# Attention scores of two shares side by side: heads of both parities in alternation, in a two-block transformer kernel

## The chip, the cores and the metric

The kernel runs on one core of a Trainium2 chip. A core has a matrix engine (TensorE, "PE" in the profile, with its weight loads shown apart as "PEld"), a vector engine (VectorE, DVE), a scalar engine (ScalarE, ACT), GpSimd (POOL) and a queue engine (SyncE, SP) that issues DMAs. TensorE writes its results to PSUM, of which the kernel uses eight banks of 512 fp32 columns. Each engine works through its own list of instructions in order, and they wait for one another on semaphores. The metric is the device time of one execution in microseconds (us).

## What is computed

The model is a stack of two blocks over 256 tokens of width 1024. The first has an RG-LRU layer and a GLA layer, each followed by a gated FFN. The second has four layers, each of FFN, mixer, FFN; the mixers are DSA, FoX, MLA and DSA again. The change concerns DSA and FoX. Cut to what matters:

```python
def dsa_mixer(x, w_in, w_out, cos_p, sin_p):
    q, k, v, qi, ki, wi = split(x @ w_in)          # 16 heads of 64; index: 8 heads of 64
    # indexer: I[t,s] = sum_h w[t,h] relu(qi[t,h] . ki[s]); keep the top 64 causal keys
    dots = einsum('bqhd,bkd->bqhk', qi, ki) * 64**-0.5
    idx_score = where(causal, einsum('bqh,bqhk->bqk', wi, relu(dots)), -inf)
    _, sel = top_k(idx_score, 64)
    logits = einsum('bqhd,bqkhd->bhqk', q, k[sel]) * 64**-0.5
    return einsum('bhqk,bqkhd->bqhd', softmax(logits), v[sel]) @ w_out

def fox_mixer(x, w_in, b_f, w_out):
    q, k, v, f = split(x @ w_in)                   # 16 heads of 64
    cum = cumsum(log_sigmoid(f + b_f))             # per head
    s = (q . k) * 64**-0.5 + cum[query] - cum[key]
    return softmax(where(causal, s, -inf)) @ v @ w_out
```

## The kernel before

**Projections.** Weights stream from HBM in 428 units of 128x2048 numbers. For each unit ScalarE rounds it (`whi`, L1025), GpSimd forms the remainder (`wlo`, L2256), and TensorE multiplies both with the activations (`hTh`, `hTl`): three fp32r matmuls for each product. L448 is the form with 256 columns, L510 that with 512. They take most of the time.

**Attention in shares.** The 16 heads times two query tiles are cut into 16 shares of two heads. Share `i` is `order[name][i]` = (t, h0) with heads h0 and h0+2, so both heads of a share have the same parity. Heads of even number lie in partitions 0 to 63 of `q` and `k`, those of odd number in 64 to 127 (`heads`). A score matmul is therefore of 64 rows; its columns are 128 for query tile t=0 and 256 for t=1. For DSA the shares go by tile (eight of t=0, then eight of t=1), for FoX two of t=0 and two of t=1 in turn. In both, shares 2m and 2m+1 have the same t and heads of opposite parity.

**A step** (`step`, L765) is `score` of share s (L714, matmuls at L723, for FoX also the bias matmul at L727 on the same 64 partitions) and `turn_share` of share s-3 (L731, fp32 transposes at L737). There are 19 steps. They stand between the projection's matmuls: `rows_units` or `chan` calls the next one after every 5, 6 or 18 of them (`beside`, `every`). After `started` steps the rest comes in `finish`, in an order written out in `tail`, with `weigh` (probabilities times values, L752) and `turn_heads_sum` (L762), and then the output projection.

**What follows a step.** VectorE's `biased` scales and masks a share and so frees its PSUM bank (L2020, FoX: two instructions L2016), then takes the row maximum (L2024). ScalarE's `exps` makes the exponentials (L1303), TensorE transposes them, and ScalarE's `turned_share` copies the result out (L1033) and frees the bank. Score banks are handed out in turn from `cb` (two banks) for DSA and from `mb` (two banks) for FoX; transposes always use `mb`. So FoX scores and transposes share two banks. `claim` makes TensorE wait until a bank's last user has freed it.

**The indexer** (`index`, L816) has 16 parts of one 64-row matmul (L825), part i being head i//2, tile i%2, one after every third L510 matmul. Each goes through a ReLU on ScalarE (L1360) and a multiply-add on VectorE (L2110), which frees the bank; they too use the two `cb` banks.

Of the kernel before, what the change touches and what calls it, by code (L numbers as in the profile page):

```python
# [14 lines left out]
P = 128  # L15
# [143 lines left out]
def program(nc, W, A2, xin, pvd, cnd, normg, adab, lng, lnb, glag, out):  # L159
    ctx = ExitStack()  # L160
    with ctx:
# [52 lines left out]
        ident = cst("ident")  # L214
# [105 lines left out]
        lag = {"dsa0": 3, "dsa1": 3, "fox": 3, "mla": 3}  # L320
# [35 lines left out]
        def steps(name):  # L356

            g = lag[name]
            return [(s if s < 16 else None, s - g if s >= g else None) for s in range(16 + g)]


        started = {"dsa0": 11, "dsa1": 11, "fox": 19, "mla": 0}

        def tail(name):


            S, W, T = (lambda *a: [("step", i) for i in a]), (lambda *a: [("weigh", i) for i in a]), lambda t, g: [("turn", t, g)]
# [12 lines left out]
            return (W(0, 1, 2, 3) + S(11) + W(4, 5, 6, 7) + S(12) + T(0, 0) + S(13) + T(0, 1) + S(14),  # L380
                    S(15) + W(8, 9) + S(16) + W(10, 11) + S(17) + W(12, 13) + T(1, 0) + S(18) + W(14, 15) + T(1, 1))


        def tensor_program(q):
# [330 lines left out]
            def score(name, i, kind, ready):  # L715

                t, h0 = order[name][i]
                nk = 128 * (t + 1)
                to = claim(bank(kind), (name, "s", i))
                ready()  # L720
                for j in range(2):
                    hd = h0 + 2 * j
                    ins = pe.matmul(to[:, j * 256:j * 256 + nk], qs[name](hd)[:, t * 128:t * 128 + 128], ks[name](hd)[:, 0:nk],  # L723
                                    start=True, stop=name != "fox")
                    if name == "fox":
                        r = 64 * (hd % 2)
                        ins = pe.matmul(to[:, j * 256:j * 256 + nk], ident[r:r + 64, r + hd:r + hd + 1].broadcast_to([64, P]),  # L727
                                        f_l[r:r + 64, 0:nk], start=False, stop=True)
                ins.then_inc(*up(s_mm, ("full", (name, "s", i))))
# [35 lines left out]
            def step(name, s, kind, ready):  # L765
                i, p = steps(name)[s]
                if i is not None:
                    score(name, i, kind, lambda: ready(i))
                if p is not None:
                    turn_share(name, p)  # L770
# [27 lines left out]
            def dsa(n, name):  # L798
# [18 lines left out]
                def index():  # L817
                    for i in range(16):
                        hd, t = i // 2, i % 2
                        o, nk = 64 * (hd % 2), 128 * (t + 1)  # L820
                        to = claim(bank("cb"), (name, "i", i))
                        q.wait_ge(*on(name, "qiT", t, 0))
                        for tt in range(t + 1):
                            q.wait_ge(*on(name, "kiT", tt, 0))
                        ins = pe.matmul(to[:, 0:nk], d_qiT3[o:o + 64, hd // 2, t * 128:t * 128 + 128], d_kiT[o:o + 64, 0:nk],  # L825
                                        start=True, stop=True)
                        ins.then_inc(*up(s_mm, ("full", (name, "i", i))))
                        yield
# [29 lines left out]
                rows_units(hi2, *hk, ready, (name, "q"), last=True, beside=beside, every=3)  # L858
# [153 lines left out]
        def scalar_program(q):  # L1012
# [302 lines left out]
            def step(name, s):  # L1315
                i, p = steps(name)[s]
                if i is not None:
                    exps(name, i)
                if p is not None:
                    turned_share(name, p)  # L1320
# [21 lines left out]
            def dsa(n, name):  # L1342
# [13 lines left out]
                def index(parts):  # L1356
                    for i in parts:
                        q.wait_ge(*on("full", (name, "i", i)))
                        to = view((name, "i", i))[:, 0:128 * (i % 2 + 1)]
                        ac.activation(to, to, ACT.Relu, scale=0.125).then_inc(*up(s_ac, (name, "relu", i)))  # L1360
# [44 lines left out]
            def fox(n, name):  # L1405
# [45 lines left out]
                step(name, 18)  # L1451
# [99 lines left out]
        def vector_program(q):  # L1551
# [475 lines left out]
            def step(name, s):  # L2027
                i, _ = steps(name)[s]
                if i is not None:
                    biased(name, i)  # L2030
# [48 lines left out]
            def dsa(n, name):  # L2079
# [20 lines left out]
                def index(parts):  # L2100
                    for i in parts:
                        hd, t = i // 2, i % 2
# [4 lines left out]
                        else:  # L2107
                            q.wait_ge(*on(name, "iadd", i - 2))
# [11 lines left out]
                for t in range(2):  # L2120
# [4 lines left out]
                    q.wait_ge(*on(name, "iadd", 14 + t))  # L2125
# [342 lines left out]
```

## Time and profile before

| what | value |
|---|---|
| runs of the kernel before | 2913.04, 2912.8, 2909.71 us; median 2912.8 |
| the profiled execution | 2909.76 us, of which the span of instructions 2908.0 us |
| mean granted TensorE clock | 0.973 |
| busy share: PE / DVE / ACT / POOL | 95% / 30% / 46% / 68% |
| score matmuls of 64 rows | DSA (L723) 128 records, FoX (L723 and L727) 128 records |
| index matmuls L825 | 64 records |
| score and transpose stages | DSA 1045 to 1110 and 2634 to 2698 us, FoX 1532 to 1630 us |

The page gives busy time for each engine; matmuls overlap, so "busy" there is an upper figure for TensorE. Where a step costs something is read in the timeline: it lists instructions by their start, merged where one follows another of its kind ("x2"), and the distance from one start to the next is what an instruction takes in the stream. An fp32 matmul leaves two records, so "L723 ... x4" is the two matmuls of one DSA share.

### The profile page before, as it was taken

The page shows a single profiled execution, that of the slowest core. Times are in us where ns is not written, and L with a number is a line of the kernel's source. Part 1 is how long each engine was busy: PE and PEld are TensorE (multiplying, and loading weights), DVE is VectorE, ACT ScalarE, POOL GpSimd, SP SyncE. Part 2 cuts the span into 40 slices and gives each one's busy share as a digit, 9 for nine tenths or more (in the row PEclk, how much of TensorE's full clock was granted, in tenths as well). Part 3 has the DMA queues.
Part 4 walks back from the last instruction along what each step waited for, and adds up shares of the span by engine and source line. Part 5 has one row for each costly group of instructions (what it writes and reads, how often), then busy time and mean ns, then how long its engine had stood idle before and what let it go on. Part 6 is the DMA issues. An engine that isn't in the chain of part 4 may idle for free.

```text
span 2908.0 us, 41508 instructions
## 1 busy us (share of the span) xinstructions
PE 2757.7 (95%) x17914; PEld 2476.6 (85%) x17914; DVE 861.8 (30%) x1464; ACT 1326.3 (46%) x1599; POOL 1970.9 (68%) x432
## 2 busy tenths in 40 slices
PE   7789988799999999999999999999799999999998
PEld 4678876699899679999988899998689999977998
DVE  6666569343200342011022200201241020143201
ACT  3554443445543454344455533433654344445443
POOL 3557754377787655878875588787538878764785
PEclk8989989899999999999999999999899999999999
DMA  8567755265555433555544355554415555443453
GB/s 326 194 258 271 253 208 192 80 215 177 184 194 183 152 131 132 188 188 194 184 179 149 121 204 188 189 188 161 158 58 212 183 199 184 169 154 116 166 184 114
DMA packets 80410, 522.12 MB, mean 180 GB/s; under 512 B 8908, under 2 KB 9292, under 8 KB 24420
## 3 DMA queue, kind: packets, MB, share of 16 engines
q1 hardware_dynamic: 80228, 519.47, 49.8%
q8 instruction: 142, 2.33, 0.3%
q14 instruction: 40, 0.33, 0.0%
HBM read 518.38 MB, written 1.05 MB: 179 GB/s over the span
## 4 chain that ended last, share of the span: by engine, by line
PE 81%; DVE 9%; ACT 6%; POOL 2%; DMA 2%; issue 1%; SPq 0%; DVEq 0%; ACTq 0%
PE cb L448 40%; PE acc L510 14%; PE acc L471 14%; PE cb L562 3%; ACT whi L1025 2%; POOL wlo L2256 2%; DVE AR L1736 1%; PE acc L752 1%; PE cb L723 1%; PE acc L448 1%; DMA raw<-in_w 1%; PE mb L737 1%; PE acc L422 1%; DVE hTl L1686 1%; ACT AR L1114 1%
## 5 line engine op out<-in xcount | busy, mean ns | idle before, releaser
L2256 POOL TENSOR_TENSOR wlo<-raw,whi 128x2048 fp32r<-128x2048 f32 x428 | 1970.7, 4613 | 913.4 <-ACT whi L1025 813.7
L1025 ACT ACTIVATE whi<-raw 128x2048 fp32r<-128x2048 f32 x428 | 817.9, 1913 | 910.0 <-PE cb L448 602.7
L448 PE MATMUL cb<-hTh,whi 128*128 128x256 f32 x3328 | 946.6, 284 | 7.9 <-DVE cb L1745 7.9
L448 PE MATMUL cb<-hTl,whi 128*128 128x256 f32 x3328 | 942.5, 283 | 0.0
L448 PE MATMUL cb<-hTh,wlo 128*128 128x256 f32 x3328 | 942.4, 283 | 0.0
L448 PEld LDWEIGHTS cb<-hTh,whi 128*128 128x128 f32 x3328 | 639.1, 192 | 16.7 <-issue 13.8
L448 PEld LDWEIGHTS cb<-hTl,whi 128*128 128x128 f32 x3328 | 639.2, 192 | 3.8 <-issue 1.2
L448 PEld LDWEIGHTS cb<-hTh,wlo 128*128 128x128 f32 x3328 | 639.3, 192 | 0.0
L471 PE MATMUL acc<-whi,ARR 128*128 128x512 f32 x1312 | 367.0, 391 | 2.7 <-DVE ARR L1686 2.7
L1749 DVE SCALAR_TENSOR_TENSOR cb<-cb,AR 128x512 f32<-128x512 f32 x80 | 56.0, 700 | 979.3 <-PE cb L448 979.3
L471 PEld LDWEIGHTS acc<-whi,ARR 128*128 128x128 f32 x1312 | 241.4, 188 | 50.7 <-issue 4.8
L471 PE MATMUL acc<-wlo,ARR 128*128 128x512 f32 x656 | 202.6, 390 | 0.0
L510 PE MATMUL acc<-whi,hTh 128*128 128x512 f32 x464 | 148.4, 400 | 13.4 <-POOL wlo L2256 8.3
L510 PE MATMUL acc<-wlo,hTh 128*128 128x512 f32 x464 | 154.5, 398 | 0.0
L510 PE MATMUL acc<-whi,ARR 128*128 128x512 f32 x512 | 143.5, 398 | 3.3 <-DVE ARR L1686 3.3
L471 PEld LDWEIGHTS acc<-wlo,ARR 128*128 128x128 f32 x656 | 123.2, 188 | 26.5
L510 PE MATMUL acc<-whi,hTl 128*128 128x512 f32 x464 | 142.9, 388 | 0.0
L510 PEld LDWEIGHTS acc<-whi,ARR 128*128 128x128 f32 x512 | 97.1, 191 | 25.7 <-issue 6.1
L1686 DVE TENSOR_TENSOR ARR<-cb,ARR 128x512 fp32r<-128x512 f32 x105 | 72.3, 689 | 153.7 <-ACT ARR L1033 153.7
L510 PEld LDWEIGHTS acc<-whi,hTh 128*128 128x128 f32 x464 | 80.2, 194 | 33.2 <-issue 15.6
L1736 DVE SCALAR_TENSOR_TENSOR AR<-cb,pv,AR 128x255 f32<-128x255 f32 (+1 forms) x144 | 66.1, 480 | 132.4 <-ACT AR L1114 129.9
L510 PEld LDWEIGHTS acc<-wlo,hTh 128*128 128x128 f32 x464 | 84.1, 192 | 16.7
(299 smaller groups left out, 3088.6 us busy)
## 6 DMA issues: line engine op xcount, KB each, us to landing
raw<-in_w SPq DMA_DIRECT2D x436, 1024.0 KB, 4.8
AR<-in_a SPq DMA_DIRECT2D x80, 512.0 KB, 5.5
gb<-in_lng SPq DMA_DIRECT2D x12, 512.0 KB, 5.7
gb<-in_lnb SPq DMA_DIRECT2D x12, 512.0 KB, 6.5
gb<-in_normg SPq DMA_DIRECT2D x8, 512.0 KB, 6.4
x<-in_x SPq DMA_DIRECT2D x1, 1024.0 KB, 9.4
out<-x SPq DMA_DIRECT2D x2, 512.0 KB, 2.7
cn<-in_cn SPq DMA_DIRECT2D x1, 560.0 KB, 7.2
```

Of the source, the lines that this page charges most:

```text
L422: ins = pe.transpose(to[:, j * 128:j * 128 + 128], src[:, t, i * 128:i * 128 + 128], ident)
L448: ins = pe.matmul(to[:, j * 256:j * 256 + 256], a[:, w], y[:, k, :], start=k == 0 and m == 0, stop=k == 7 and m == 2)
L471: ins = pe.matmul(acc[:, 2 * t + c, 0:c1 - c0], xs[y], a[:, kk * width + c0:kk * width + c1], start=first and kk == 0 and m == 0, stop=las ...
L510: ins = pe.matmul(acc[:, 2 * t + c, 0:c1 - c0], xs[y], a[:, kk * width + c0:kk * width + c1], start=first and i == 0 and kk == 0 and m == ...
L562: ins = pe.matmul(to[:, i * 256:i * 256 + 256], y[:, k, tk], a[:, k * 256:k * 256 + 256], start=k == 0 and m == 0, stop=k == 7 and m == 2)
L723: ins = pe.matmul(to[:, j * 256:j * 256 + nk], qs[name](hd)[:, t * 128:t * 128 + 128], ks[name](hd)[:, 0:nk], start=True, stop=name != "fox")
L737: ins = pe.transpose(to[:, m * 128:m * 128 + 128], s3[:, j, kt * 128:kt * 128 + 128], ident)
L1025: ac.activation(whi[i % NH][:, :], raw[u % NR][:, :], ACT.Copy).then_inc(*up(s_hi, ("hi", i)))
L1686: dv.tensor_tensor(dst, src, high.bitcast(F32), ALU.subtract).then_inc(*up(s_dv, *names))
L1736: dv.scalar_tensor_tensor(out=to[:, a + sh:a + 256], in0=view(key)[:, a:a + 256 - sh], scalar=pvc(w, (2 - sh) * 44 + c0 + j), in1=to[:, a ...
L1749: dv.scalar_tensor_tensor(out=view(key1), in0=view(key1), scalar=0.5, in1=tmp(0, p % 2), op0=ALU.mult, op1=ALU.mult).then_inc(*up(s_dv, (" ...
L2256: po.tensor_tensor(wlo[i % NH][:, :], raw[(i + NADA) % NR][:, :], whi[i % NH][:, :].bitcast(F32), ALU.subtract).then_inc(*up(s_lo, ("lo", i)))
```

## The change

The diff, cut to its core:

```diff
-        lag = {"dsa0": 3, "dsa1": 3, "fox": 3, "mla": 3}
+        paired = {"dsa0": True, "dsa1": True, "fox": True, "mla": False}
...
         def steps(name):
-            g = lag[name]
-            return [(s if s < 16 else None, s - g if s >= g else None) for s in range(16 + g)]
-        started = {"dsa0": 11, "dsa1": 11, "fox": 19, "mla": 0}
+            if paired[name]:
+                return [((s, s + 1) if s % 2 == 0 and s < 16 else (), (s - 3, s - 2) if s % 2 and s > 2 else ())
+                        for s in range(18)]
+            return [((s,) if s < 16 else (), (s - 3,) if s > 2 else ()) for s in range(19)]
+        def index_part(i):
+            return i // 4 * 2 + i % 2, i // 2 % 2
+        started = {"dsa0": 11, "dsa1": 11, "fox": 18, "mla": 0}
...
-            def score(name, i, kind, ready):
-                t, h0 = order[name][i]
-                nk = 128 * (t + 1)
-                to = claim(bank(kind), (name, "s", i))
-                ready()
+            def scores_of(name, parts, kind, ready):
+                to = [claim(bank(kind), (name, "s", i)) for i in parts]
+                for i in parts:
+                    ready(i)
                 for j in range(2):
-                    hd = h0 + 2 * j
-                    ins = pe.matmul(to[:, j * 256:j * 256 + nk], qs[name](hd)[:, t * 128:t * 128 + 128], ks[name](hd)[:, 0:nk],
-                                    start=True, stop=name != "fox")
+                    for i, o in zip(parts, to):
+                        t, h0 = order[name][i]
+                        hd, nk = h0 + 2 * j, 128 * (t + 1)
+                        ins = pe.matmul(o[:, j * 256:j * 256 + nk], qs[name](hd)[:, t * 128:t * 128 + 128], ks[name](hd)[:, 0:nk],
+                                        start=True, stop=name != "fox")
...
-                ins.then_inc(*up(s_mm, ("full", (name, "s", i))))
+                ins.then_inc(*up(s_mm, *[("full", (name, "s", i)) for i in parts]))
...
-                    for i in range(16):
-                        hd, t = i // 2, i % 2
-                        o, nk = 64 * (hd % 2), 128 * (t + 1)
-                        to = claim(bank("cb"), (name, "i", i))
+                    for i0 in range(0, 16, 2):
+                        to = [claim(bank("cb"), (name, "i", i)) for i in (i0, i0 + 1)]
+                        for i in (i0, i0 + 1):
+                            hd, t = index_part(i)
...
-                rows_units(hi2, *hk, ready, (name, "q"), last=True, beside=beside, every=3)
+                rows_units(hi2, *hk, ready, (name, "q"), last=True, beside=beside, every=6)
```

Even steps now hold the scores of two shares, odd steps the transposes of two; `scores_of` claims both banks of the ring at once, goes through the two heads of each share in alternation of the shares, and reports both as full after its last matmul. The indexer takes two heads of one tile together, after every sixth matmul. VectorE and ScalarE follow the same steps; their instructions are the same, the multiply-adds of the indexer in the new order of parts. MLA, GpSimd's list and the DMA queue's list are as before. `tail` loses its last step for DSA.

TensorE in FoX, `mb0` and `mb1` being the two banks, L448 (after: L455) the matmuls of a channel unit. Before, share 3 with the transposes of share 0:

```order
L448 MATMUL cb<-hTh,wlo1 128x256
L723 MATMUL mb1<-AR 128x256 [waits s_dv]
L727 MATMUL mb1<-AR,cn 128x256
L723 MATMUL mb1<-AR 128x256
L727 MATMUL mb1<-AR,cn 128x256
L737 MATMUL mb0<-cn,AR 128x128 [waits s_ac,s_dv]
L737 MATMUL mb0<-cn,AR 128x128
L448 MATMUL cb<-hTh,whi1 128x256
```
After, shares 4 and 5 in one piece:

```order
L455 MATMUL cb<-hTh,wlo2 128x256
L732 MATMUL mb0<-AR 128x128 [waits s_ac]
L732 MATMUL mb1<-AR 128x128
L739 MATMUL mb0<-AR,cn 128x128
L739 MATMUL mb1<-AR,cn 128x128
L732 MATMUL mb0<-AR 128x128
L732 MATMUL mb1<-AR 128x128
L739 MATMUL mb0<-AR,cn 128x128
L739 MATMUL mb1<-AR,cn 128x128
L455 MATMUL cb<-hTh,whi2 128x256
```
The score rows of two shares have moved together and alternate in bank, and so in parity. The transposes have moved to a place of their own, 18 channel matmuls behind; here are those of shares 2 and 3:

```order
L455 MATMUL cb<-hTh,wlo2 128x256
L749 MATMUL mb0<-cn,AR 128x128 [waits s_dv]
L749 MATMUL mb0<-cn,AR 128x128 x3
L749 MATMUL mb1<-cn,AR 128x128 [waits s_dv]
L749 MATMUL mb1<-cn,AR 128x128 x3
L455 MATMUL cb<-hTh,whi2 128x256
```
They have moved behind the next pair's scores and claim the two banks that these have just filled, each with a wait for VectorE.

TensorE in the indexer of the first DSA layer, between L510 (after: L517) matmuls. Before:

```order
L825 MATMUL cb<-AR 128x256 [waits s_ac,s_dv]
L510 MATMUL acc<-whi3,hTh 128x512 x2
L510 MATMUL acc<-wlo3,hTh 128x512
L825 MATMUL cb<-AR 128x128 [waits s_dv]
L510 MATMUL acc<-wlo3,hTh 128x512
L510 MATMUL acc<-whi3,hTl 128x512 x2
L825 MATMUL cb<-AR 128x256 [waits s_dv]
```
Each part stands alone, three matmuls from the next. After:

```order
L838 MATMUL cb<-AR 128x128 x2
L517 MATMUL acc<-whi3,hTh 128x512 x2
L517 MATMUL acc<-wlo3,hTh 128x512 x2
L517 MATMUL acc<-whi3,hTl 128x512 x2
L838 MATMUL cb<-AR 128x256 [waits s_ac,s_dv]
L838 MATMUL cb<-AR 128x256
```
Parts have moved from every third matmul to two after every sixth, both of one width.

TensorE in the tail of the first DSA layer, up to the output projection at L510 (after: L517). Before, from the first `turn_heads_sum` (L762), with shares 13 and 14 at L723 and the transposes of shares 10 and 11 at L737:

```order
L762 MATMUL mb0<-cn,AR 128x128 [waits s_dv,s_ac]
L762 MATMUL mb0<-cn,AR 128x128 x3
L723 MATMUL cb<-AR 128x256 [waits s_dv]
L723 MATMUL cb<-AR 128x256
L737 MATMUL mb1<-cn,AR 128x128 [waits s_ac]
L737 MATMUL mb1<-cn,AR 128x128 x3
L762 MATMUL mb0<-cn,AR 128x128 [waits s_dv]
L762 MATMUL mb0<-cn,AR 128x128 x3
L723 MATMUL cb<-AR 128x256 x2
L737 MATMUL mb1<-cn,AR 128x128 [waits s_ac]
L737 MATMUL mb1<-cn,AR 128x128 x3
L510 MATMUL acc<-whi1,hTh 128x512 [waits s_lo,s_hi]
```
Scores and transposes stand between the two `turn_heads_sum`. After (L732 scores, L749 transposes, L774 `turn_heads_sum`), from the scores of shares 12 and 13:

```order
L732 MATMUL cb<-AR 128x256 [waits s_dv]
L732 MATMUL cb<-AR 128x256 x3
L774 MATMUL mb0<-cn,AR 128x128 [waits s_dv,s_ac]
L774 MATMUL mb0<-cn,AR 128x128 x3
L749 MATMUL mb1<-cn,AR 128x128 [waits s_ac]
L749 MATMUL mb1<-cn,AR 128x128 x3
L749 MATMUL mb0<-cn,AR 128x128 [waits s_dv]
L749 MATMUL mb0<-cn,AR 128x128 x3
L774 MATMUL mb1<-cn,AR 128x128 [waits s_ac]
L774 MATMUL mb1<-cn,AR 128x128 x3
L732 MATMUL cb<-AR 128x256 x4
L517 MATMUL acc<-whi1,hTh 128x512 [waits s_lo,s_hi]
```
Shares 12 and 13 have moved ahead of the first `turn_heads_sum`, 14 and 15 behind the second, and the transposes of shares 10 and 11 both stand between the two, the second of them with a wait for VectorE.

## Rows read from the trace of the kernel before

**Rows 1.** The page, part 4: the chain that ended last, by engine.
```profile
PE 81%; DVE 9%; ACT 6%; POOL 2%; DMA 2%; issue 1%; SPq 0%; DVEq 0%; ACTq 0%
```

**Rows 2.** Timeline of TensorE, DSA, 128-column scores: start, us, engine, line, tiles, count.
```profile
1046.97 0.62 PE L510 MATMUL acc<-whi,hTh 128*128 128x512 f32 x2
1047.52 0.71 PE L723 MATMUL cb<-AR 64*128 64x128 f32 x4
1048.16 0.73 PE L510 MATMUL acc<-wlo,hTh 128*128 128x512 f32 x2
1048.72 0.62 PE L510 MATMUL acc<-whi,hTl 128*128 128x512 f32 x2
1049.19 0.62 PE L510 MATMUL acc<-whi,hTh 128*128 128x512 f32 x2
```

**Rows 3.** Timeline of TensorE, FoX, a 256-column share between channel matmuls.
```profile
1540.92 0.28 PE L448 MATMUL cb<-hTh,wlo 128*128 128x256 f32 x1
1541.13 0.70 PE L723 MATMUL mb<-AR 64*128 64x256 f32 x2
1541.66 0.59 PE L727 MATMUL mb<-AR,cn 64*128 64x256 f32 x2
1542.10 0.59 PE L723 MATMUL mb<-AR 64*128 64x256 f32 x2
...
1543.05 0.39 PE L448 MATMUL cb<-hTh,whi 128*128 128x256 f32 x1
1543.27 0.28 PE L448 MATMUL cb<-hTl,whi 128*128 128x256 f32 x1
```

**Rows 4.** Timeline of TensorE, indexer: the 128-column parts of two heads.
```profile
994.70 0.48 PE L825 MATMUL cb<-AR 64*128 64x128 f32 x2
...
997.53 0.48 PE L825 MATMUL cb<-AR 64*128 64x128 f32 x2
```

**Rows 5.** Timeline of TensorE, FoX: matmuls of 64 columns in a run.
```profile
1608.45 7.26 PE L752 MATMUL acc<-z,AR 128*128 128x64 f32 x64
1615.54 1.04 PE L762 MATMUL mb<-cn,AR 128*128 128x128 f32 x8
```

**Rows 6.** Timeline of ScalarE in the indexer; the bracket is idle time before, and its releaser.
```profile
1001.70 1.02 ACT L1033 ACTIVATE AR<-acc 128x1024 f32<-128x1024 f32 x1 [1.75 <-DVE acc L2077]
...
1005.37 0.37 ACT L1360 ACTIVATE cb<-cb 128x256 f32<-128x256 f32 x1 [1.25 <-PE cb L825]
```

**Rows 7.** Timeline of VectorE, FoX, one 256-column share.
```profile
1543.16 0.88 DVE L2016 SCALAR_TENSOR_TENSOR AR<-mb,AR,cn 128x256 f32<-128x256 f32 x2 [4.64 <-PE mb L727]
1544.07 0.69 DVE L2024 TENSOR_REDUCE sm<-AR 128x2 f32<-128x512 f32 x1
```

**Rows 8.** Timeline of TensorE, first DSA layer, share 8 to the output projection.
```profile
1063.26 1.13 PE L723 MATMUL cb<-AR 64*128 64x256 f32 x4
...
1079.89 0.66 PE L737 MATMUL mb<-cn,AR 128*128 128x128 f32 x4 [1.03 <-ACT AR L1033]
...
1084.03 1.11 PE L737 MATMUL mb<-cn,AR 128*128 128x128 f32 x4 [0.74 <-ACT AR L1033]
1084.80 1.20 PE L510 MATMUL acc<-whi,hTh 128*128 128x512 f32 x2
```

**Rows 9.** Timeline of ScalarE in the same tail.
```profile
1072.30 1.90 ACT L1025 ACTIVATE whi<-raw 128x2048 fp32r<-128x2048 f32 x1
1074.10 1.01 ACT L1033 ACTIVATE z<-acc 128x1024 f32<-128x1024 f32 x1
1075.01 0.50 ACT L1303 ACTIVATE AR<-AR,sm 128x256 f32<-128x256 f32 x1
...
1075.99 0.58 ACT L1033 ACTIVATE AR<-mb 128x512 f32<-128x512 f32 x1
```

**Rows 10.** Timeline of VectorE in the same tail, one share.
```profile
1073.44 0.69 DVE L2020 SCALAR_TENSOR_TENSOR AR<-cb,AR 128x512 f32<-128x512 f32 x1
1074.17 0.69 DVE L2024 TENSOR_REDUCE sm<-AR 128x2 f32<-128x512 f32 x1
```

**Rows 11.** Windows: length, busy of PE, PEld, DVE, ACT, POOL, granted clock, DMA.
```profile
1082.00:1092.00 10.00, 9.26 (x30) 6.61 (x28) 3.73 (x6) 5.20 (x16) 0.00 (x0) 0.51 0.10 42
2672.50:2679.50 7.00, 6.58 (x19) 4.71 (x20) 3.35 (x5) 3.12 (x10) 0.00 (x0) 0.52 0.00 0
```

More of the change, by code:

```diff
@@ L713, in gla @@
                 out_units(n, lh, ll, ready)
-            def score(name, i, kind, ready):
-                t, h0 = order[name][i]
-                nk = 128 * (t + 1)
-                to = claim(bank(kind), (name, "s", i))
-                ready()
-                for j in range(2):
-                    hd = h0 + 2 * j
-                    ins = pe.matmul(to[:, j * 256:j * 256 + nk], qs[name](hd)[:, t * 128:t * 128 + 128], ks[name](hd)[:, 0:nk],
-                                    start=True, stop=name != "fox")
-                    if name == "fox":
-                        r = 64 * (hd % 2)
-                        ins = pe.matmul(to[:, j * 256:j * 256 + nk], ident[r:r + 64, r + hd:r + hd + 1].broadcast_to([64, P]),
-                                        f_l[r:r + 64, 0:nk], start=False, stop=True)
-                ins.then_inc(*up(s_mm, ("full", (name, "s", i))))
+            def scores_of(name, parts, kind, ready):
+                to = [claim(bank(kind), (name, "s", i)) for i in parts]
+                for i in parts:
+                    ready(i)
+                for j in range(2):
+                    for i, o in zip(parts, to):
[3 more added lines that the diff above has]
+                                        start=True, stop=name != "fox")
+                    if name == "fox":
+                        for i, o in zip(parts, to):
+                            t, h0 = order[name][i]
+                            hd, nk = h0 + 2 * j, 128 * (t + 1)
+                            r = 64 * (hd % 2)
+                            ins = pe.matmul(o[:, j * 256:j * 256 + nk], ident[r:r + 64, r + hd:r + hd + 1].broadcast_to([64, P]),
+                                            f_l[r:r + 64, 0:nk], start=False, stop=True)
+                ins.then_inc(*up(s_mm, *[("full", (name, "s", i)) for i in parts]))
             def turn_share(name, i):
@@ L765, in step @@
             def step(name, s, kind, ready):
[L766 to L769, printed above, removed]
+                scores, turns = steps(name)[s]
+                if scores:
+                    scores_of(name, scores, kind, ready)
+                for p in turns:
                     turn_share(name, p)
@@ L817, in index @@
                 def index():
-                    for i in range(16):
-                        hd, t = i // 2, i % 2
-                        o, nk = 64 * (hd % 2), 128 * (t + 1)
-                        to = claim(bank("cb"), (name, "i", i))
[L822 to L827, printed above, removed]
+                    for i0 in range(0, 16, 2):
+                        to = [claim(bank("cb"), (name, "i", i)) for i in (i0, i0 + 1)]
+                        for i in (i0, i0 + 1):
+                            hd, t = index_part(i)
+                            o, nk = 64 * (hd % 2), 128 * (t + 1)
+                            q.wait_ge(*on(name, "qiT", t, 0))
+                            for tt in range(t + 1):
+                                q.wait_ge(*on(name, "kiT", tt, 0))
+                            ins = pe.matmul(to[i % 2][:, 0:nk], d_qiT3[o:o + 64, hd // 2, t * 128:t * 128 + 128],
+                                            d_kiT[o:o + 64, 0:nk], start=True, stop=True)
+                        ins.then_inc(*up(s_mm, ("full", (name, "i", i0)), ("full", (name, "i", i0 + 1))))
                         yield
@@ L1315, in step @@
             def step(name, s):
-                i, p = steps(name)[s]
-                if i is not None:
+                scores, turns = steps(name)[s]
+                for i in scores:
                     exps(name, i)
-                if p is not None:
+                for p in turns:
                     turned_share(name, p)
@@ L2027, in step @@
             def step(name, s):
-                i, _ = steps(name)[s]
-                if i is not None:
+                for i in steps(name)[s][0]:
                     biased(name, i)
```

11 lines of the change are left out of this document (5 added, 6 removed).

## Prediction

> **What bounds the kernel now.** I read the chain that ended last first: 81% of it is TensorE [rows 1]. The timelines of the changed stages then show how: between the projection's matmuls the other engines are rarely waited for, and the time of a score is what its matmuls, and the gaps around them, take out of TensorE's stream. Only the tail of a DSA layer has waits, 1.03 us on ScalarE among them [rows 8]. So a saving in TensorE's stream should reach the end, unless a new wait takes it back.
>
> **The gap around a score.** DSA, 128 columns: from the L510 pair at 1046.97 to the one at 1048.72 are 1.75 us [rows 2]. Two L510 pairs in them take 0.47 each (1048.72 to 1049.19). That leaves 0.81 for four records of scores. What is a record? In FoX, 256 columns, two records take 0.44 (1541.66 to 1542.10) [rows 3], so 0.217 each and, by columns, 0.108 at 128. Four are 0.43, and 0.38 is left for going in and out. FoX gives the same: 1540.92 to 1543.05 is 2.13, less 0.12 for an L448 and 8 x 0.217 = 1.74, leaves 0.27, and the next L448 comes 0.22 later, not 0.12: together 0.37. The indexer too: two parts have a period of 2.83 [rows 4]; six L510 take 1.40, two records at 128 and two at 256 columns 0.65; 0.78 is left for two, 0.39 each. I take **0.38 us** for every stretch of 64-row matmuls between 128-row ones.
>
> **Removed.** Stretches: in each DSA layer 16 index parts become 8 pairs and 16 scores 8 pairs, in FoX 16 scores 8 pairs. That is 16 + 16 + 8 = 40 stretches fewer, 40 x 0.38 = **15.2 us**. What hid a gap? Nothing; all lie in TensorE's stream. The number of matmuls and transposes is the same, and transposes show no such gap of their own worth counting: I set their pairing at nothing.
>
> The Trainium skill says the same of the gap and more: "TensorEngine Tiling (Array Packing)", Key Properties, has the engine drain when the tiling mode changes, though not when only the tile does. The first half agrees with the 0.38; no row here shows the second.
>
> **Perhaps overlapped.** Alternation puts matmuls on the two halves of the array side by side. No row of before has such neighbours, so I bound it. At the low end nothing overlaps. At the high end the last record of one share runs beside the first of the other: a DSA pair of 8 records takes 5 slots, a FoX pair of 16 takes 9, an index pair of 4 takes 3. But weight loads go one after another: 64 records of only 64 columns take 7.09 us, 0.111 each [rows 5], which is what loads then allow. At 128 columns (0.108 a record) the loads leave no gain. So at 256 columns only: DSA 2 layers x 4 pairs x 3 x 0.217 = 5.2, FoX 4 x 7 x 0.217 = 6.1, index 2 x 4 x 0.217 = 1.7, in all 13.0. In between: the load for the other half starts only when the matmul ahead of it has started, and so comes 0.11 late, which halves the gain to 6.5. I take the **middle**, as every load in these rows keeps just one matmul ahead.
>
> **Added waits.** A pair claims both banks at once, and a bank is free only when its share has gone through the other engines.
> - Indexer. After the fourth pair VectorE turns q (until ScalarE's 1.02 us copy of q may start, 1001.70 [rows 6]); ScalarE's ReLU of the fifth pair stands behind that copy. Fourth pair ends at 0; two ReLUs (0.37 first) and two multiply-adds until 1.35; rotation 1.3, until 2.65; copy until 3.7; two ReLUs and two multiply-adds until 4.75. TensorE, free of the fifth pair at 2.1, has 1.4 of matmuls and the entry: it asks at 3.7. **Wait 1.1**, twice: 2.2 us. Before, with one part in each bank, it asked in this place no earlier than it was answered.
> - FoX. Two 256-column shares: mask 0.88, maximum 0.69, mask 0.88 [rows 7], with the first start 0.1 after the scores: second bank free at 2.65. TensorE asks for it after 18 L448 (2.16) and two transposes (0.2): 0.3, three times. In the last stretch only six L510 (1.4) stand between: 1.0 there, and 0.5 for the pair behind it, which waits for ScalarE's copies. Together **2.4 us**. Queued behind these waits are the projection's matmuls.
> - DSA tail. Walk from share 8 (0, at 1063.26 [rows 8]), a 256-column pair being 2.1 without overlap: shares 10, 11 end at 6.8, 12, 13 at 14.2. ScalarE must first make the exponentials of 10 and 11 (about 1.0 a share with its sums, 1075.01 to 1075.99), round a unit (1.90) and copy the values (1.01) [rows 9], so share 8's copy comes at 14.3. The first `turn_heads_sum` is done at 14.9. Its copy stands behind the exponentials of 12 and 13, whose maxima come at 15.65 and 17.1 (1.45 a share [rows 10]): copied 18.8, freed by VectorE 19.5. Only then share 11's transposes, the second `turn_heads_sum`, and shares 14, 15: output projection at 22.6. Before it began at 21.5 (1084.80), some 0.9 of it from the slow clock, and share 15 (1.2) was still to come: 21.9. So the tail loses 0.7 where the sum above gave it 4 x 0.38 = 1.5: **2.2 a layer, 4.4 us**. With half overlap the same walk gives 21.3: 1.3 better a layer, which is what the middle contains; I keep 5.2 / 2 = 2.6 for both.
>
> Every other engine's work is the same, and GpSimd and the DMAs have no moved row.
>
> **Clock.** In both tails the granted clock is at 1.2 GHz, 0.51 and 0.52 in the windows, for 10 and 7 us [rows 11], after the waits of rows 8. The new wait for share 11's bank, some 3.5 us in one, would do the same about as late. I leave the loss equal and give it plus or minus 3 us a layer.
>
> **Sum.** 15.2 - 2.2 - 2.4 - 4.4 + 6.5 = **12.7 us**, from the profiled 2909.8 to 2897.1. The three runs shown lie from 2909.7 to 2913.0, median 2912.8, so the profiled one is a low one; I add 1.5, half the way to the median, for the same in the runs after: **2898.6**. About 0.2% (5.8 us) is what a measurement of this kernel can tell from no change.
>
> **Rivals.**
> - *No overlap.* 15.2 - 9.0 = 6.2: **2905**. For it: no row shows two matmuls at once. Against: they write different banks and read different partitions.
> - *Full overlap at 256 columns.* 19.2 saved: **2892**; if loads for the two halves also ran side by side, the 128-column pairs would add as much as half again, 6.5: **2885**. This is what the Trainium skill expects: "TensorE: Matmul & The Clock Gate", Part 3, has matmuls of different row groups run concurrently, a few ns apart, and weight loads overlap with matmuls of another group. No row of before can show it.
> - *Slower: each change of half drains the array*, as a change between 128 and 64 rows does. Half of 0.38 is 0.19 a change; a DSA pair has 3, a FoX pair 7, an index pair 1: 48 + 56 + 16 = 120 changes, 22.8 us, against 6.2 saved: 16.6 slower, **2928**. It decides from 0.05 us a change. Against it: inside a 64-row stretch records follow at 0.22, nothing lost [rows 3]; but there the half never changes.
> - *It does not do what it says*: pairs fall apart at a wait in the middle. The order speaks against it: only the first row of a pair waits.
>
> **How the numbers follow.** Middle overlap 0.33, full or more 0.27, none 0.22, draining 0.10, the rest (waits eat all, near 2911) 0.08. The clock's 3 us a layer blurs each. The range takes in full overlap and none: **2885 to 2908**. Faster by over 0.2% (under some 2906): 0.33 + 0.27 + most of none, 0.78. Same 0.11, slower 0.11.
>
> **What would show it.** Right: 40 fewer stretches with the gap of 0.38; a DSA 256-column pair from last L510 to next in about 1.8 us over the L510 themselves (2.1: no overlap, 1.5: full, 2.7: draining); FoX pairs 3.1 (3.9, 2.3, 5.2). Waits on VectorE of about 1 us at the fifth index pair and at the last FoX transposes, and one of 3 us or more at the transposes in the DSA tail, with the clock down behind it. Wrong: a clock that stays down through the whole output projection, or waits for `whi` or `wlo` where there were none.

## The result

| kernel | runs, us | median |
|---|---|---|
| before | 2913.04, 2912.8, 2909.71, 2909.77 | 2911.28 |
| after | 2876.25, 2875.47, 2873.31, 2876.74 | **2875.86** |

The ratio is 0.9877, with a 95% interval of 0.986 to 0.9894: 35 us less, where the prediction had 2898.6 and a range from 2885 to 2908. The sign was right, the size was not: the gain is nearly three times the 12.7 us of the sum. The profiled execution after took 2876.25 us, its span 2874.4 (before 2908.0), 33.6 us less. One run of a later kernel (the order six, two, two, six below) took 3025.62 us at a granted clock of 0.834, a slower state of the chip, and is left out.

The chain that ended last, from the page of after, is TensorE's as before [rows 1]:

```profile
PE 80%; DVE 9%; ACT 6%; DMA 2%; POOL 2%; issue 1%; SPq 0%; DVEq 0%; ACTq 0%
```

TensorE in the first DSA layer after, a pair of 128 columns and one of 256 (start, us, engine, line, tiles, count):

```profile
1047.94 0.39 PE L517 MATMUL acc<-whi,hTl 128*128 128x512 f32 x1
1048.26 0.72 PE L732 MATMUL cb<-AR 64*128 64x128 f32 x8
1048.90 0.50 PE L517 MATMUL acc<-whi,hTl 128*128 128x512 f32 x1
...
1058.75 0.40 PE L517 MATMUL acc<-whi,hTl 128*128 128x512 f32 x1
1059.08 1.13 PE L732 MATMUL cb<-AR 64*128 64x256 f32 x8
1060.14 0.50 PE L517 MATMUL acc<-whi,hTl 128*128 128x512 f32 x1
```

From the first score record to the next L517 are 0.64 and 1.06 us. Before, one share of 128 columns, with 4 records, took the same 0.64 (1047.52 to 1048.16, [rows 2]), and one of 256 took 1.06: it starts at 1063.26 in [rows 8], and the next row of TensorE there, a transpose, is

```profile
1064.32 0.44 PE L737 MATMUL mb<-cn,AR 128*128 128x128 f32 x2
```

**A pair takes the time of one share**: eight records in four slots, at 128 columns too (a slot is the distance from one record to the next, 0.108 us at 128 columns and 0.217 at 256). All the pairs do so: an index pair takes 0.42 and 0.63 us, where one part took 0.41 and 0.63. FoX shows the same (timeline of after, a 256-column pair):

```profile
1530.57 0.28 PE L455 MATMUL cb<-hTh,wlo 128*128 128x256 f32 x1
1530.78 0.70 PE L732 MATMUL mb<-AR 64*128 64x256 f32 x4
1531.32 0.60 PE L739 MATMUL mb<-AR,cn 64*128 64x256 f32 x4
1531.75 0.60 PE L732 MATMUL mb<-AR 64*128 64x256 f32 x4
1532.18 0.60 PE L739 MATMUL mb<-AR,cn 64*128 64x256 f32 x4
1532.71 0.39 PE L455 MATMUL cb<-hTh,whi 128*128 128x256 f32 x1
```

The starts have the distances of one share before [rows 3], now with four records in each where there were two. The weight loads run together as well. All eight of the 256-column DSA pair lie in one merged stretch of 0.73 us:

```profile
1059.07 0.73 PEld L732 LDWEIGHTS cb<-AR 64*128 64x128 f32 x8 [0.36 <-issue]
```

Seen in narrower windows they start two at a time, at 1059.07, 1059.18, 1059.40 and 1059.61, where matmuls of 128 rows in a run, each with its load, come one in every 0.11 [rows 5].

TensorE's waits after, in the indexer, in FoX and in the first DSA tail (bracket: idle time before, and what ended it):

```profile
1004.63 0.70 PE L838 MATMUL cb<-AR 64*128 64x256 f32 x4 [1.20 <-DVE AR L2121]
...
1576.40 0.70 PE L732 MATMUL mb<-AR 64*128 64x256 f32 x4 [0.24 <-ACT AR L1046]
...
1071.66 0.66 PE L774 MATMUL mb<-cn,AR 128*128 128x128 f32 x4 [1.14 <-ACT AR L1046]
1075.69 1.11 PE L749 MATMUL mb<-cn,AR 128*128 128x128 f32 x4 [2.89 <-DVE hTl L1698]
```

They stand where the prediction put them. The granted clock goes down at the last one. Windows of after, one in each DSA tail (length, busy of PE, PEld, DVE, ACT, POOL, granted clock, DMA), which answer to [rows 11]:

```profile
1074.00:1082.00 8.00, 6.31 (x26) 4.76 (x27) 3.60 (x6) 3.43 (x9) 1.04 (x1) 0.57 0.46 170
2641.00:2645.00 4.00, 4.00 (x18) 2.65 (x17) 1.97 (x3) 1.08 (x2) 0.00 (x0) 0.57 0.67 246
```

One minus the clock, times the length, is what a window loses: 3.4 and 1.7 us here, 4.9 (5.1 with its edges) and 3.4 in rows 11 of before.

**The account.** Three rows with a wait of 2.8 us for `wlo`, which the change does not touch, cut the span into pieces: one ahead of the first DSA layer (A), one behind FoX (B), one ahead of the second DSA layer (C).

| kernel | start to A | A to B | B to C | C to end | A to B and C to end | lost to the clock in the two DSA tails |
|---|---|---|---|---|---|---|
| before | 962.6 | 1071.9 | 516.6 | 356.8 | 1428.7 | 8.5 |
| after | 965.3 | 1048.4 | 516.4 | 344.4 | 1392.7 | 5.1 |

The changed pieces lost 36.0 us; the first piece, with the same instructions, came 2.7 later in this execution. By rows: half the stretches of scores and index parts are gone whole, 8.2 us in each DSA layer for scores (4 x 0.82 + 4 x 1.25, the 0.2 for entry and exit in them), 5.6 for index parts, 13.5 in FoX: 41.2. New waits take back 2.7 in the indexers (1.20, 0.27 and 1.19), 0.4 in FoX, 2.9 in the two tails (4.03 and 4.02 of waits, less the 2.33 and 2.79 that were there). The clock gives 3.4. That makes 38.6, 2.6 more than measured; those 2.6 I have not placed.

### The profile page after: what moved, and what is told of

It is laid out like the page before. It is cut to its first block, busy times and chain, and to the rows that moved or that the text cites. A ratio compares the mean times of both kernels' runs of the same rounds, so it can differ in the third digit from the quotient of the medians.

```text
span 2874.4 us, 41530 instructions
## 1 busy us (share of the span) xinstructions
PE 2716.0 (94%) x17914; PEld 2454.7 (85%) x17914; DVE 860.3 (30%) x1464; ACT 1324.7 (46%) x1599; POOL 1970.7 (69%) x432
## 3 DMA queue, kind: packets, MB, share of 16 engines
q8 instruction: 142, 2.33, 0.3%
## 4 chain that ended last, share of the span: by engine, by line
PE 80%; DVE 9%; ACT 6%; DMA 2%; POOL 2%; issue 1%; SPq 0%; DVEq 0%; ACTq 0%
PE cb L455 41%; PE acc L478 14%; PE acc L517 13%; PE cb L569 3%; ACT whi L1038 2%; POOL wlo L2267 2%; DVE AR L1748 1%; PE acc L764 1%; PE acc L455 1%; DMA AR<-in_a 1%; DMA raw<-in_w 1%; PE acc L429 1%; PE cb L732 1%; DVE hTl L1698 1%; ACT AR L1127 1%
## 5 line engine op out<-in xcount | busy, mean ns | idle before, releaser
L455 PE MATMUL cb<-hTh,whi 128*128 128x256 f32 x3328 | 947.6, 285 | 7.9 <-DVE cb L1757 7.9
L455 PE MATMUL cb<-hTh,wlo 128*128 128x256 f32 x3328 | 943.1, 283 | 0.0
L455 PE MATMUL cb<-hTl,whi 128*128 128x256 f32 x3328 | 943.1, 283 | 0.0
L455 PEld LDWEIGHTS cb<-hTh,whi 128*128 128x128 f32 x3328 | 640.0, 192 | 17.7 <-issue 14.7
L455 PEld LDWEIGHTS cb<-hTl,whi 128*128 128x128 f32 x3328 | 639.9, 192 | 4.1 <-issue 1.5
L455 PEld LDWEIGHTS cb<-hTh,wlo 128*128 128x128 f32 x3328 | 639.8, 192 | 0.0
L517 PE MATMUL acc<-whi,hTh 128*128 128x512 f32 x464 | 147.8, 399 | 13.4 <-POOL wlo L2267 8.3
L517 PE MATMUL acc<-wlo,hTh 128*128 128x512 f32 x464 | 149.3, 392 | 0.0
L517 PE MATMUL acc<-whi,ARR 128*128 128x512 f32 x512 | 143.3, 398 | 3.3 <-DVE ARR L1698 3.3
L517 PE MATMUL acc<-whi,hTl 128*128 128x512 f32 x464 | 141.9, 385 | 0.0
L517 PEld LDWEIGHTS acc<-whi,ARR 128*128 128x128 f32 x512 | 97.1, 191 | 25.7 <-issue 6.1
L517 PEld LDWEIGHTS acc<-whi,hTh 128*128 128x128 f32 x464 | 80.3, 193 | 33.9 <-issue 14.5
L517 PEld LDWEIGHTS acc<-wlo,hTh 128*128 128x128 f32 x464 | 83.9, 192 | 16.3 <-issue 0.7
```

Source lines behind the costliest of these rows:

```text
L455: ins = pe.matmul(to[:, j * 256:j * 256 + 256], a[:, w], y[:, k, :], start=k == 0 and m == 0, stop=k == 7 and m == 2)
L517: ins = pe.matmul(acc[:, 2 * t + c, 0:c1 - c0], xs[y], a[:, kk * width + c0:kk * width + c1], start=first and i == 0 and kk == 0 and m == ...
```

## Experiments

The theory after the result: the two halves of the array work at once, loads and matmuls (26 of the 41.2 us), and fewer stretches save the gaps (15.2). Both numbers are worked out from the lengths of the pairs. The rival: fewer stretches and handshakes save it all.

**The same half in both shares.** DSA's pairs and the index pairs are made of heads of one parity.

```diff
+        by_parity = [(t, 4 * (qq + dq) + o) for t in range(2) for qq in (0, 2) for o in range(2) for dq in range(2)]
-        order = {"dsa0": by_tile, "dsa1": by_tile, "mla": by_tile, "fox": by_head}
+        order = {"dsa0": by_parity, "dsa1": by_parity, "mla": by_tile, "fox": by_head}
...
-            return i // 4 * 2 + i % 2, i // 2 % 2
+            return i // 8 * 4 + i // 4 % 2 + 2 * (i % 2), i // 2 % 2
...
```

VectorE's waits from one multiply-add of the indexer to the next follow the new order of parts (left out of the diff).

> The changed kernel, except that in the DSA layers the two shares of a pair, and the two index parts of a pair, use heads of the same parity, so the same 64 rows of the array. FoX stays in alternation. Nothing is left out of the computation. Theory A (the two halves of the array run side by side, weight loads too): this takes the overlap away. A DSA pair of 8 records then takes 8 slots instead of 4: 0.43 us longer at 128 columns (8 pairs in the two layers), 0.87 at 256 (8 pairs), an index pair 0.22 and 0.43 (8 each). Sum 3.5 + 6.9 + 1.7 + 3.5 = 15.6 us, less some 2 that the waits in the indexer and in the tail hide: 12 to 16 us slower than the changed kernel, about 2889. The 256-column DSA pair takes 2.1 us instead of 1.1. Rival B (the gain came from fewer stretches, and from fewer claims and waits per share; the halves add nothing): no more than 1 us from the changed kernel, about 2876.

Measured: 2891.58 us (0.9932, 0.9917 to 0.9947), 15.7 above after. In the changed pieces of the span it is 17.9, of which 5.1 are the clock in the DSA tails; the 12.8 left stand against the 12 to 16 expected. Its 256-column pair:

```profile
1059.29 0.40 PE L518 MATMUL acc<-whi,hTl 128*128 128x512 f32 x1
1059.62 1.99 PE L733 MATMUL cb<-AR 64*128 64x256 f32 x8
1061.54 0.50 PE L518 MATMUL acc<-whi,hTl 128*128 128x512 f32 x1
```

1.92 us, where the pair of both parities takes 1.06 with the same records, handshakes and waits. The rival falls for DSA and the indexer; FoX was not run with one parity, and rests on its pairs' lengths here and in the next runs. The pair of 128 columns takes 1.09 instead of 0.64; with the 0.09 and 0.10 on its sides it is 1.28, and two single shares are 2 x 0.82, so a stretch saved is worth 0.36: the gap of the prediction.

**Each share in a block.** In `scores_of` the loops over shares and heads change places.

```diff
-                for j in range(2):
-                    for i, o in zip(parts, to):
+                for i, o in zip(parts, to):
+                    for j in range(2):
...
```

> The changed kernel with the same pairs in the same stretches, but in each pair all matmuls of the first share are issued before all of the second, instead of in alternation. The index pairs (one matmul each) are as they were. Nothing is left out. Theory A1 (the two halves overlap only where neighbours in the instruction stream use different halves, because the engine starts matmuls in order): of a DSA pair only the middle overlaps, 8 records take 7 slots instead of 4, 3 x 0.108 at 128 columns and 3 x 0.217 at 256, 8 pairs each: 2.6 + 5.2; a FoX pair of 16 takes 15 instead of 8, 7 slots: 4 x 0.76 + 4 x 1.52 = 9.1. Together 16.9 us slower, about 2892. Theory A2 (each half has a queue of its own that the other does not hold up): as the changed kernel, 2876, within 1.5 us. Between them, a queue that looks ahead by one or two records would give a middle value, and the starts of the records in the trace would show it.

Measured: 2880.92 (0.9894, 0.9878 to 0.9911), 5.1 above after: between the theories. The DSA pair (runs of four records) loses nothing, the FoX pair (runs of eight) does:

```profile
1056.88 1.14 PE L732 MATMUL cb<-AR 64*128 64x256 f32 x8
1057.95 0.50 PE L517 MATMUL acc<-whi,hTl 128*128 128x512 f32 x1
...
1529.27 0.70 PE L732 MATMUL mb<-AR 64*128 64x256 f32 x2
1529.81 0.59 PE L736 MATMUL mb<-AR,cn 64*128 64x256 f32 x2
1530.24 0.70 PE L732 MATMUL mb<-AR 64*128 64x256 f32 x4
1530.67 0.70 PE L736 MATMUL mb<-AR,cn 64*128 64x256 f32 x4
1531.21 0.59 PE L732 MATMUL mb<-AR 64*128 64x256 f32 x2
1531.64 0.59 PE L736 MATMUL mb<-AR,cn 64*128 64x256 f32 x2
1532.16 0.39 PE L455 MATMUL cb<-hTh,whi 128*128 128x256 f32 x1
```

Two records at 1529.27 and two at 1529.81 run alone; then every start has two, then the last four run alone: 12 slots, 2.89 us instead of 1.93, and 1.64 instead of 1.09 at 128 columns. The second share starts when four records of the first have not. (More exactly, its first record starts within 0.01 us behind the fifth of the first share, with three behind that; four counts the one that it starts beside.) That the order of starts is not that of the program, the line numbers show: at 1530.24 the first share has two records at L732 left, and four come before the next at L736. This is a new theory L: a matmul may start on its idle half while up to four records of the other half, ahead of it in the program, have not started. Two more orders of a FoX pair test the number four.

**Runs of four in FoX.**

```diff
-                    if name == "fox":
-                        for i, o in zip(parts, to):
-                            t, h0 = order[name][i]
-                            hd, nk = h0 + 2 * j, 128 * (t + 1)
+                        if name == "fox":
...
```

> The changed kernel, except that in a FoX pair each share's score and bias matmul of a head come together before the other share's: runs of 4 records of one half (0, 1, 0, 1) instead of runs of 2. Nothing is left out. Block order (runs of 8) showed a FoX pair of 12 slots where alternation shows 8, and a DSA pair (runs of 4) with nothing lost. Theory L (a matmul may start on its idle half when up to 4 records of the other half, ahead of it in the program, have not): 8 slots, the same time as the changed kernel, 2875 within 1.5 us, a 256-column FoX pair of 1.93 us from its first record to the next projection matmul. Rival (only direct neighbours overlap, and the DSA pair escaped for some other reason): 3 ends between runs overlap, 16 records take 13 slots: 5 x (4 x 0.108 + 4 x 0.217) = 6.5 us slower, a 256-column pair of 3.0 us.

**Six, two, two, six.** The matmuls (share, head, score or bias) in the order:

```diff
+                    for x, j, m in ((0, 0, 0), (0, 0, 1), (0, 1, 0), (1, 0, 0), (0, 1, 1), (1, 0, 1), (1, 1, 0), (1, 1, 1)):
+                        ins = one(x, j, bool(m))
```

> The changed kernel with another order in a FoX pair: share A's first three matmuls (6 records), B's first (2), A's last (2), B's last three (6). Nothing is left out. Theory L with its 4 records: B's first starts when 4 of A's first six are left, 2 slots late, and the rest of B follows without a hole, so 10 slots: by the 6.0 us that block order (12 slots) cost in FoX's part of the span, 3.0 us more than the changed kernel, about 2878, and a 256-column pair of 2.4 us, one of 128 columns of 1.35. If the limit were 2 records: 12 slots, 6 us more and 2.9 us a pair; if none: 8 slots, nothing more.

Measured: 2875.63 (0.9878, 0.9863 to 0.9894) and 2878.14 (0.9889, 0.9869 to 0.9909), expected 2875 and 2878. The times alone are too close for their intervals of about 5 us each; the pairs decide. They take 1.19 and 2.03 us with runs of four (0.1 more than in alternation, against 3.0 for the rival), 1.42 and 2.46 with six, two, two, six (expected 1.35 and 2.4). In the second, the other share's score starts beside the first share's bias, when two records of the first run of six are past and three are still to come:

```profile
1529.07 0.70 PE L734 MATMUL mb<-AR 64*128 64x256 f32 x2
1529.60 0.38 PE L734 MATMUL mb<-AR,cn 64*128 64x256 f32 x1
1529.61 0.48 PE L734 MATMUL mb<-AR 64*128 64x256 f32 x1
```

Theory L holds for these four orders. Whether four counts records or fp32 matmuls (two of them), they do not tell; nor what the limit is on, matmuls or their loads.

**One part of the change alone.** `paired` is false for the others, or the index parts are as before, with the waits and the tail that go with it.

> The kernel before with one part of the change alone: the index parts in pairs of both parities in alternation. Scores of DSA and FoX as before. Nothing is left out. By the account of the two traces (a gap of 0.38 us gone per pair and full overlap, 5.6 a layer, less the new wait of 1.2 and some 0.5 of others) the stretch of the index parts is 3.9 us shorter in each layer: 7.8 us, ratio to the kernel before 0.9973. If overlap were worth nothing: 2 x (3.0 - 1.7) = 2.6 us, 0.9991.

> The kernel before with one part of the change alone: FoX's scores in pairs, with the transposes of two shares together. DSA as before. Nothing is left out. By the account of the two traces: 13.5 us less in the stretches of scores, less waits of 0.2 to 1.5: 12 to 13 us, ratio to the kernel before 0.9957. If only the gaps were saved: 8 x 0.38 = 3.0 less the waits, 2 us, 0.9993.

> The kernel before with one part of the change alone: DSA's scores in pairs of both parities in alternation. Index parts and FoX as before. Nothing is left out. By the account of the two traces: the stretches of scores are 8.2 us shorter in each layer, and the new waits in the tail (1.1 and 2.9) cost 4.0, of which a shorter time at the low clock gives 1 to 2 back: 2 x 5 to 6, 10 to 13 us less, ratio to the kernel before 0.9960. The other two parts alone measured 9.1 and 15.4, so if the three do not disturb each other, 35.4 - 24.5 = 10.9. If only the gaps were saved and the waits cost what I had worked out: 1.7 us.

| part alone | median | ratio, 95% | saved | expected | A to B and C to end |
|---|---|---|---|---|---|
| index | 2902.29 | 0.9968, 0.9955 to 0.9981 | 9.1 | 7.8 | 8.6 |
| FoX | 2895.99 | 0.9947, 0.9932 to 0.9962 | 15.4 | 12 to 13 | 12.7 |
| DSA scores | 2897.03 | 0.9951, 0.9938 to 0.9965 | 14.2 | 10 to 13 | 16.0 |

Each part saves several times what its gaps, less its waits, would give. All three came out above what was expected. For DSA scores there is a reason: 4.0 us a layer were taken off for the waits in the tail, though 2.33 and 2.79 us of waits stood there before. With 2.9 in all taken off and 3.4 added for the clock, 16.4 of pairs give 16.9, near the 16.0 of the last column. The sum, 38.7, is 2.0 above the 36.7 of the whole as measured beside the third part (2911.25 less 2874.54); with intervals of about 4 us each, the parts add up.

**The waits in the tail.** The rest concerns the price of the waits.

> The changed kernel once more, word for word, as the neighbour of the runs of this call on the same chip: 2876, ratio to the kernel before 0.988.

Measured: 2874.54 (0.9874, 0.9861 to 0.9888).

```diff
-            return (W(0, 1, 2, 3) + S(11) + W(4, 5, 6, 7) + S(12) + T(0, 0) + S(13) + T(0, 1) + S(14),
-                    S(15) + W(8, 9) + S(16) + W(10, 11) + S(17) + W(12, 13) + T(1, 0) + W(14, 15) + T(1, 1))
+            return (W(0, 1, 2, 3) + S(11) + W(4, 5, 6, 7) + T(0, 0) + S(12) + S(13),
+                    S(14) + S(16) + T(0, 1) + S(15) + W(8, 9, 10, 11) + S(17) + W(12, 13) + T(1, 0) + W(14, 15) + T(1, 1))
...
```

The part left out lets ScalarE copy the values and round its unit earlier in `finish`.

> The changed kernel with another order in the tail of the DSA layers: the first transposes of a heads' sum before the pair of shares 12 and 13, the output projection begun before the last pair, the last transposes and the second heads' sum beside it; ScalarE copies the values and rounds its unit so much earlier. Nothing is left out. Theory W (the 1.14 and 2.89 us at the bank of shares 8 to 11 are waits for ScalarE's and VectorE's place in line, and the low clock of some 6 us at half speed is their consequence): the waits go, 4.0 us a layer, and with them part of the 3 us that the clock costs: 5 to 7 us a layer, 10 to 14 us less than the changed kernel, about 2864. Theory V (VectorE's and ScalarE's work on the last shares is the bound of the tail, so the wait only moves to the output projection, for hTl or AR): 0 to 3 us less, 2873 to 2876, with the same 3 to 4 us of waits a layer at other lines.

Measured: 2875.41 (0.9873, 0.9853 to 0.9892), no gain; its runs lie from 2866.9 to 2884.1. The next kernel has the same tail and this in ScalarE's indexer:

```diff
-                index(range(8))
+                index(range(10))
                 sum_out(d_q, "q", on(name, "qrope", 0), 0)
-                index(range(8, 12))
+                index(range(10, 12))
```

> The tail of the kernel above, and in the indexer ScalarE's ReLU of the fifth index pair ahead of its copy of q. Nothing is left out. If the wait of 1.20 us at the fifth index pair comes only from the ReLU's place behind the copy, this takes 1.2 us a layer off the kernel above, 2.4 us in all, about 2861 if theory W holds. If VectorE's rotation of q is the late one instead, the wait stays at 1.2 and nothing is saved.

Measured: 2872.81 (0.9866, 0.9853 to 0.988). The 1.2 us at the fifth index pair are gone, so they were the ReLU's place in line, but the tail gave nothing. Its waits show why. TensorE with the new tail, in the first and the second DSA layer of the first of these two kernels, and the windows behind the waits:

```profile
1073.39 1.14 PE L732 MATMUL cb<-AR 64*128 64x256 f32 x8 [0.65 <-DVE AR L2034]
1079.67 0.66 PE L749 MATMUL mb<-cn,AR 128*128 128x128 f32 x4 [1.99 <-DVE hTl L1700]
```

```profile
1081.00:1095.00 14.00, 14.00 (x56) 12.60 (x55) 0.90 (x2) 1.18 (x2) 0.00 (x0) 0.51 0.02 9
2648.00:2662.00 14.00, 13.96 (x97) 12.71 (x97) 1.32 (x3) 3.77 (x6) 0.00 (x0) 1.00 0.12 48
```

The waits of a layer fell from 4.0 to 2.6 us, and the second layer has the same two (0.66 and 1.98). But behind the same wait the clock stood at 0.51, 1.2 GHz, for 14 us in one layer, with TensorE busy all the time, and at 1.00 in the other. The kernel with both edits shows it the other way round (1.00 in the first layer, 0.52 in the second). So a wait of 2 us costs either itself or 6.8 us more. The clock is tied to the waits more loosely than theory W has it: it fell in before too, behind waits of at most 1.21 us, and after itself, measured again, lost 3.4 us in its second tail behind the same 2.9 that cost it 1.7 the first time. And the new order took too little of the waits away. Hence a third order, in which both heads' sums are transposed before the last pair, and on ScalarE the copies of shares 10 and 11 and of the second sum stand ahead of the exponentials:

```diff
+            return (W(0, 1, 2, 3) + S(11) + W(4, 5, 6, 7) + T(0, 0) + S(12) + S(13),
+                    T(0, 1) + S(14) + W(8, 9) + S(15) + W(10, 11) + S(17) + W(12, 13) + T(1, 0) + W(14, 15) + T(1, 1))
...
+                    before, rest = before[:-2] + [("step", 13), rest[0], ("step", 12)], rest[1:]
```

> The changed kernel with ScalarE's ReLU of the fifth index pair ahead of its copy of q, and the tail of the DSA layers in a third order: both heads' sums transposed before the last pair of shares, the output projection begun before it, and ScalarE's copies of shares 10 and 11 and of the second heads' sum ahead of the exponentials of shares 12 to 15. Nothing is left out. In the second order a wait of 0.65 and one of 2.0 us stayed, the latter for the bank of the second heads' sum, behind 4 exponentials of the last pair; with the clock lost for 6.8 us in one layer and not at all in the other. Theory W (the waits are places in line, and the clock falls only behind a wait of that size): both waits go below 0.7 us, the clock stays up in both layers, and 3 us of waits and 6.8 us of clock go: about 2864. Theory V (ScalarE and VectorE are the bound of the tail): 2 us or more of waits a layer stay at other lines and the time stays at 2872.

Measured: **2858.3** (0.982, 0.9805 to 0.9834), its runs from 2856.9 to 2859.1: 16.2 us below after (2874.54, with 2911.25 for before beside it), and 52.5 below before (2910.84 beside this one). That is 6 us less than expected. Two of the six are waits: 3 us were counted on, and in the tails 4.9 went (5.3 of the kernel with both edits became 0.4). The rest I have not placed. TensorE's waits in its first DSA tail, and both tails in windows:

```profile
1070.65 0.66 PE L774 MATMUL mb<-cn,AR 128*128 128x128 f32 x4 [0.21 <-ACT AR L1046]
...
1091.20 0.66 PE L774 MATMUL mb<-cn,AR 128*128 128x128 f32 x4 [0.27 <-DVE AR L2055]
```

```profile
1066.00:1096.00 30.00, 29.52 (x190) 24.69 (x190) 12.13 (x21) 15.89 (x34) 6.65 (x2) 1.00 0.20 71
2621.00:2651.00 30.00, 29.52 (x190) 24.65 (x190) 12.25 (x22) 15.87 (x35) 6.51 (x2) 1.00 0.19 70
```

Theory V falls: nothing but order was changed, the 4.0 us of waits a layer became 0.2 (the 0.27 stood in after too), and the clock is up in both layers. In the changed pieces of the span it is 15.2 us less than after: 7.6 of waits in the tails, 2.7 in the indexers and 5.1 of clock make 15.4. Whether this order alone would have helped the kernel before, which has waits and a low clock in the same tails, was not tried.

## Why the prediction was wrong

**The step that failed is "Perhaps overlapped".** It put full overlap at 13.0 us and took half of it, 6.5; the lengths of the pairs give 26 (41.2 less the 15.2 of the gaps). Three choices in it were wrong, each against the gain:
- *"Weight loads go one after another."* Rows 5 are matmuls of 128 rows in a run, each with its load; they say nothing on loads for two different halves. Those run together, so the 128-column pairs gain as much as the others. The step's "loads leave no gain" at 128 columns had no row behind it; 0.64 us for eight records refutes it.
- *"A DSA pair takes 5 slots, a FoX pair 9, an index pair 3."* They take 4, 8 and 2. The second share does not start one slot late.
- *The middle, as "every load in these rows keeps just one matmul ahead".* Within one share the traces show that. The block orders show that a matmul for the idle half starts beside a record of the other and ahead of up to three more.

The text named the case that came ("if loads for the two halves also ran side by side", 2885), but still on 5, 9 and 3 slots and with only "half as much again" for 128 columns. With 26 in the place of 6.5 and nothing else touched the sum is 32.2, and the time 2877.6 by the profiled run, 1.4 from what it took. That this is so near is partly luck: the waits were 3.0 less and the clock 3.4 better than in the sum, while the first piece of the span came 2.7 later and 2.6 are not placed. The 1.5 added because the profiled run of before was a low one had no counterpart: after took 2876.25 profiled, with a median of 2875.86. The page named there, the Trainium skill's "TensorE: Matmul & The Clock Gate", Part 3, is borne out: matmuls of different row groups ran together. I gave the row more weight than the page (0.33 to 0.27), and the row did not bear on the question.

**The gap around a score: right.** 0.38 forecast; 0.36 by the pair of one parity.

**Waits.** Indexer: 1.1 forecast, 1.20 and 1.19, and one of 0.27 that was not. FoX: 0.3 three times, 1.0 and 0.5 forecast, which is 2.4; measured none, 0.66 and 0.24, and 0.47 that was there before is gone, which leaves 0.4. Tail: the walk had the places right, and its "some 3.5 us" for share 11's bank was 2.89; the two tails lost 2.9 in waits where I had 4.4 with the gaps counted. Together 6.0 for 9.0.

**The clock: a term set equal that was not.** It came out 3.4 us better, by luck as the runs of the tail show, and within the 3 us a layer allowed for.

**Rivals.** No overlap and draining at each change of half fall with the first trace: a 256-column pair takes 1.25 us over the L517 themselves (1058.75 to 1060.47, less two of 0.235), against 2.1 and 2.7. Pairs did not fall apart at a wait either: no idle time stands inside a pair.

## What to carry to other kernels

When two fp32 matmuls of 64 rows can go to different halves of the array and different banks, count them as one, loads included; runs of up to four records per half cost at most 0.1 us a pair here, and need no finer alternation. A row read from one queue does not bound what two independent halves do; ask first whether the row could show the effect at all. And after a stretch gets shorter, look at the order of the engines that serve it: here some 15 us lay in a few waits for banks and in the clock behind them, and another order alone gave them back.

## What the runs showed of the hardware

- **Matmuls start out of program order across halves.** The Trainium skill, "TensorE: Matmul & The Clock Gate", Part 2, says that matmuls stay in program order and only weight loads are pulled ahead. In block order the second share's scores start beside the first share's, from the fifth record in FoX (1530.24) and from the first in DSA (eight records in 1.07 us), and so ahead of three records that stand before them in the program. The measurement decides.
- **One and the same wait is followed by different losses of clock.** A wait of 2.0 us, with one of 0.65 us ahead of it, was followed by no loss in two tails and by 6.8 us in two. The two waits of after (1.1 and 2.9 us) were followed by 3.4 and 1.7 us in one execution and by 3.4 twice in another. Before, with no wait over 1.21 us, the two tails lost 5.1 and 3.4. Only the order with waits of 0.2 us lost nothing in both tails. The runs of the two kernels with the 2.0 us wait are up to 17 and 10 us apart, those of after 3 to 5, those of the kernel without such waits 2.2; that the clock is what spreads them is argued and not shown, as one execution of each set was profiled.
- Both parities in one bank, which would need no pairing, was not tried: the Trainium skill, "TensorEngine Tiling (Array Packing)", Gotcha 1, says that different row tiles cannot access one PSUM bank at the same time. No run here shows it.
